# Two matmuls a block instead of three: high weights against both activation parts at once, and a VectorE sum over pairs

## The reference, cut to what matters

```
p = h @ w_in                         # RWKV inputs; then the recurrence
x = x + gt1 * (mix @ w_out)
y = conv3(h @ w_up); x = x + gt2 * ((silu(gate) * val) @ w_down)
z = u @ w_in_2                       # q, k, v, conv branch, gates
h = h + (g_a * (y_a @ w_out_a) + g_b * (att @ w_o_attn)) @ w_mix_out
... a second conv feed-forward, and a final norm
```

## Time and profile before

| | |
|---|---|
| median of 3 runs | 2957.46 us (2954.05 to 2957.95) |
| profiled execution | 2959.5 us from its first to its last instruction |
| TensorE busy | 2802.0 us (95%) |
| TensorE weight loads busy | 2634.0 us (89%) |
| VectorE busy | 1603.0 us (54%) |
| ScalarE busy | 1261.7 us (43%) |
| GpSimd busy | 154.5 us (5%) |
| HBM | 551.29 MB read, 187 GB/s over the span |
| chain that ended last | PE 64%, issue 27%, DVE 4%, DMA 3%, POOL 1%, ACT 1% |

### The profile page before, as it was taken

How to read it: one execution, slowest core, us unless ns; L and a number is a source line. 1 busy time by engine, 2 the same in 40 slices (tenths; PEclk the granted TensorE clock), 3 DMA queues, 4 the chain that set the end, 5 groups by cost and what they waited for, 6 DMA issues and landing times.

```text
span 2959.5 us, 61527 instructions
## 1 busy us (share of the span) xinstructions
PE 2802.0 (95%) x24076; PEld 2634.0 (89%) x24076; DVE 1603.0 (54%) x2138; ACT 1261.7 (43%) x1697; POOL 154.5 (5%) x159
## 2 busy tenths in 40 slices
PE   5799898889899999999979999999989999999997
PEld 0477777769899999999979999999989999999997
DVE  0445454534666666655554565556466666665444
ACT  1432222124555555544434345654455555554443
POOL 1001101131000000001110000000100000000000
PEclk8799999969899999999989999999999999999998
DMA  9675555405345555555545544445535555555553
GB/s 404 274 297 215 214 216 213 193 26 180 138 181 184 184 183 181 178 184 197 201 148 184 180 164 157 159 166 184 184 143 183 184 184 182 177 181 183 199 199 113
DMA packets 76132, 554.88 MB, mean 187 GB/s; under 512 B 8448, under 2 KB 8576, under 8 KB 9088
## 3 DMA queue, kind: packets, MB, share of 16 engines
q1 hardware_dynamic: 75456, 549.16, 50.6%
q10 hardware_dynamic: 432, 2.16, 0.2%
q0 software_dynamic: 144, 2.10, 0.2%
HBM read 551.29 MB, written 2.10 MB: 187 GB/s over the span
## 4 chain that ended last, share of the span: by engine, by line
PE 64%; issue 27%; DVE 4%; DMA 3%; POOL 1%; ACT 1%; DVEq 0%; SPq 0%; POOLq 0%; ACTq 0%
PE bank L428 18%; PE bank L430 18%; PE bank L429 18%; DMA raw<-in_stream_dram 3%; PE bank L461 2%; PE bank L577 1%; PE bank L591 1%; PE bank L587 1%; PE bank L672 1%; PE bank L540 1%; POOL ssq L1750 1%; DVE wlo L1235 0%; POOL wssq L1747 0%; PE bank L644 0%; PE bank L648 0%
## 5 line engine op out<-in xcount | busy, mean ns | idle before, releaser
L428 PE MATMUL bank<-ahi,whi 128*128 128x256 f32 x4976 | 1434.8, 288 | 53.4 <-DVE alo L1263 36.0
L429 PE MATMUL bank<-alo,whi 128*128 128x256 f32 x4976 | 1416.1, 285 | 0.0
L430 PE MATMUL bank<-ahi,wlo 128*128 128x256 f32 x4976 | 1415.6, 284 | 0.0
L1235 DVE TENSOR_TENSOR wlo<-raw,whi 128x1024 fp32r<-128x1024 f32 x846 | 1027.4, 1228 | 262.3 <-ACT whi L889 257.2
L889 ACT ACTIVATE whi<-raw 128x1024 fp32r<-128x1024 f32 x846 | 892.0, 1055 | 572.0 <-PE bank L430 459.7
L428 PEld LDWEIGHTS bank<-ahi,whi 128*128 128x128 f32 x4976 | 962.5, 193 | 85.8 <-issue 69.5
L429 PEld LDWEIGHTS bank<-alo,whi 128*128 128x128 f32 x4976 | 963.6, 194 | 2.8 <-issue 2.6
L430 PEld LDWEIGHTS bank<-ahi,wlo 128*128 128x128 f32 x4976 | 963.2, 194 | 0.0
L428 PE MATMUL bank<-ffhi,whi 128*128 128x256 f32 x1408 | 400.5, 284 | 8.3 <-DVE fflo L1541 8.3
L430 PE MATMUL bank<-ffhi,wlo 128*128 128x256 f32 x1408 | 398.6, 283 | 0.0
L429 PE MATMUL bank<-fflo,whi 128*128 128x256 f32 x1408 | 398.4, 283 | 0.0
(11 more groups left out here) (227 smaller groups left out, 1666.5 us busy)
## 6 DMA issues: line engine op xcount, KB each, us to landing
raw<-in_stream_dram SPq DMA_DIRECT2D x519, 1024.0 KB, 4.8
x<-in_x_dram SPq DMA_DIRECT2D x1, 2048.0 KB, 13.3
out_dram<-x POOLq DMA_DIRECT2D x1, 2048.0 KB, 6.7
lora_w<-in_lora_dram SPq DMA_DIRECT2D x1, 1536.0 KB, 11.2
pool_w<-in_pool_w_dram ACTq DMA_DIRECT2D x1, 1024.0 KB, 9.4
catt<-in_att_dram ACTq DMA_DIRECT2D x1, 576.0 KB, 3.8
par<-in_params_dram SPq DMA_DIRECT2D x1, 541.5 KB, 3.9
pool_inv<-in_pool_inv_dram ACTq DMA_DIRECT2D x1, 512.0 KB, 14.0
```

The source lines that it names most:

```text
L428: nc.tensor.matmul(tile_bank(t), wh, hi[:, kt], start=starts and n == 0, stop=False)
L429: nc.tensor.matmul(tile_bank(t), wh, lo[:, kt], start=False, stop=False)
L430: mm = nc.tensor.matmul(tile_bank(t), wl, hi[:, kt], start=False, stop=stops and last)
L1235: nc.vector.tensor_tensor(wlo[:, k % RING], raw[:, r % RING, 8 * (k % 2):8 * (k % 2) + 8], whi[:, k % RING].bitcast(F32), ALU.subtract).th ...
```

## The change

The high and low activation parts of one feature tile now lie side by side (`act2`, `ff2`, `ya2`, `oa2`), so that one matmul of 512 columns multiplies the high weights with both; it fills a whole bank. The low weights times the high part go into the bank's second half. A tile is the sum of the two halves, so whatever read a tile from PSUM now needs a sum: VectorE's `join` adds the halves, as a reduction over pairs that lie 256 values apart, into SBUF (`joined` or the final place), and the operations behind it read that. In `residual_tile`, two operations take the place of one instead. The bank is given back with the join (`tile_sum`). In `up` ScalarE's and VectorE's taps move one step later, behind the join, and read SBUF; silu, gate, high and low move by a step. `down` waits for the hidden tiles in three portions.

```diff
+        act2 = sb("act2", [P, KT, 2, T], F32R)
+        ahi, alo = act2[:, :, 0], act2[:, :, 1]
...
-                    nc.tensor.matmul(tile_bank(t), wh, hi[:, kt], start=starts and n == 0, stop=False)
-                    nc.tensor.matmul(tile_bank(t), wh, lo[:, kt], start=False, stop=False)
-                    mm = nc.tensor.matmul(tile_bank(t), wl, hi[:, kt], start=False, stop=stops and last)
+                    nc.tensor.matmul(tile_bank(t), wh, flat(pair[:, kt]), start=starts and n == 0, stop=False)
+                    mm = nc.tensor.matmul(small_half(t), wl, pair[:, kt, 0], start=False, stop=stops and last)
...
-                    pe.wait_ge(tile_free, t + 1 - banks + dt * i)
+                    pe.wait_ge(tile_sum, t + 1 - banks + dt * i)
...  down, TensorE
                         for c in range(3):
+                            if j == 0:
+                                pe.wait_ge(ff_ready, which * NF + min(DKT * c + DKT, NF))
...
-            pe.wait_ge(ff_ready, NF)
-            down("down1")
+            down("down1", 0)
...  VectorE
+            def join(dst, phase, j, i=0, per=0):
+                dve.wait_ge(half_used, 2 * FIRST_CHUNK[phase] + (j + 1) * HALVES[phase] + HALVES[phase] * per * i)
+                halves = tile_bank(FIRST_TILE[phase] + j).rearrange("p (h t) -> p t h", h=2)
+                nc.vector.tensor_reduce(dst, halves, AX.X, ALU.add).then_inc(tile_sum, 1)
...  wkv_body, VectorE, step n
-                    if n % 2 == 1 and n // 2 < 6:
-                        j = n // 2
+                    j = n // 2
+                    if n % 2 == 1:
+                        t = FIRST_TILE["wkv"] + j
+                        join(joined[:, t % 2] if j < 6 else one(mix, NR + j - 6 + 2 * i), "wkv", j, i, 8)
+                    if n % 2 == 1 and j < 6:
                         dve.wait_ge(scaled, SCALED["wkv"] + j + 1 + 6 * i)
...  wkv, ScalarE
-                    nc.scalar.activation(dst, tile_bank(t), ACT.Identity, scale=col(om_mu, 3 + 8 * (j // 2) + j % 2 + 2 * i))\
-                        .then_inc(scaled, 1)
-                else:
-                    nc.scalar.activation(one(mix, NR + j - 6 + 2 * i), tile_bank(t), ACT.Copy).then_inc(tile_free, 1)
+                act.wait_ge(tile_sum, t + 1 + 8 * i)
+                nc.scalar.activation(dst, joined[:, t % 2], ACT.Identity, scale=col(om_mu, 3 + 8 * (j // 2) + j % 2 + 2 * i))\
...  residual_tile
+                link(add(small_half(t)))
+                add(large_half(t)).then_inc(tile_sum, 1)
...  up, VectorE
                     for n in range(8):
                         lead(phase, n, i, 4)
+                        if n % 2 == 1:
+                            join(joined[:, n // 2 % 2], phase, n // 2, i, 4)
+                        elif n:
+                            taps_of(n // 2 - 1, i)
...  ao, VectorE
-                    nc.vector.tensor_tensor(yb[:, 2 * part + n % 2], tile_bank(t), one(gates, ct + KT * (n % 2)), ALU.mult)\
-                        .then_inc(tile_free, 1)
+                    join(yb[:, 2 * part + n % 2], "ao", n, i, 8)
+                    dve.wait_ge(tile_sum, t + 1 + 8 * i)
+                    link(nc.vector.tensor_tensor(yb[:, 2 * part + n % 2], yb[:, 2 * part + n % 2], one(gates, ct + KT * (n % 2)),
+                                                 ALU.mult))
```

More of the change, by code:

```diff
@@ L87 @@
     _n += TILES[_name]
+HALVES = {"lora": 2, "wkv": 2, "up1": 2, "qkv": 2, "cvb": 2, "gates": 2, "ao": 1, "up2": 2}
 PARAMS = [("c", KT), ("b_ada", 6 * KT), ("norm1_g", KT), ("mu", 27), ("w0", NR), ("a0", NR), ("k_k", NR), ("k_a", NR),
@@ L416, in _, with product @@
         def _(pe):
-            def product(k, i, dh, t, blocks, hi, lo, starts, stops, ready=None):
+            def product(k, i, dh, t, blocks, pair, starts, stops, ready=None):
                 pe.wait_ge(lo_ready, k + 1 + dh * i)
@@ L864, in _ @@
                     tile_wait(t, i, 8)
-                    hi, lo = (yahi, yalo) if n % 2 == 0 else (oahi, oalo)
-                    product(k, i, 8, t, [(b, b) for b in range(8)], hi, lo, True, True)
+                    pair = ya2 if n % 2 == 0 else oa2
+                    product(k, i, 8, t, [(b, b) for b in range(8)], pair, True, True)
             loop("mix", 4, 4, "gmix")
@@ L869, in _ @@
             loop("up2", 4, 22, "u2")
-            pe.wait_ge(ff_ready, 2 * NF)
-            down("down2")
+            down("down2", 1)
             stat("x5")
@@ L1542, in low, with taps_of @@
                                             ALU.subtract).then_inc(ff_ready, 1)
+                def taps_of(j, i):
+                    dve.wait_ge(scaled, SCALED[phase] + j + 1 + 4 * i)
+                    for m, (tap, back) in enumerate(taps):
+                        dst, src = (slice(back, T), slice(0, T - back)) if back > 0 else (slice(0, T + back), slice(-back, T))
+                        ins = nc.vector.scalar_tensor_tensor(out=yb[:, j, dst], in0=joined[:, j % 2, src],
+                                                             scalar=pcol(conv, 3 * j + tap + 12 * i), in1=yb[:, j, dst],
+                                                             op0=ALU.mult, op1=ALU.add)
+                        if m == 0:
+                            link(ins)
+                    ins.then_inc(tapped, 1)
                 def body(i, first=False):
@@ L1694, in body @@
                         cut_lo(2 * FIRST_CHUNK["gates"] + 32 * kv + n + 2, i, 8, 4)
+                        if n % 2 == 1:
+                            j = 16 * kv + n // 2
+                            join(one(gates, j + 4 * i), "gates", j, i, 4)
                         attend(n, i, kv)
```

165 lines of the change are left out of this document (81 added, 84 removed).

## The result

The changed kernel takes 2919.1 us (median of 4 runs, 2914.2 to 2930.1) where the kernel before took 2957.5 (median of 3 runs, 2954.1 to 2958.0): ratio 0.988, 95% interval 0.985 to 0.990. A fourth run of the kernel before took 5393.7 us and is left out. The changed kernel is faster by 1.2%, not by the forecast 4.7%, and lies outside the range. The profiled execution has a span of 2928.3 us.

A forecast was written before the change was run, and what follows sets the result against it. TensorE's matmul rhythm was taken to bound the dense phases. Terms -138 (blocks), -2.5 (`wkv`), -11 (`up` to `down`), +9 (`ao`), +1.6 (`gates`), +2 (tails) gave -139 from 2959.5: 2820.5, median 2818 us; range 2785 to 2895.

The forecast's parts named there:

- What a block costs: Dense phases: a block falls from 360 to 336 ns, 24 less; over 5760 blocks 138 us off.
- I take that for the new matmul of 512 columns: Block price: the 0.216 us between plain float32 matmuls is taken as the float32r cost at 512 columns.
- 13 ns of the 120 are something else: 256-column matmuls: columns alone would take 107 ns at full clock; the rest was put down to the longer, overlapping weight load.
- a fixed 13 ns per matmul: Rival on block cost, chance 0.15: a block saves 13.3 ns, 77 us in all, time 2885.
- the prediction is wrong if 512 columns take over 0.227: Failure sign for the dense phases: a 512-column matmul was expected to be followed after 0.216 us.
- the half clock: Objection to the fixed-cost rival: at 1.2 GHz 256-column matmuls follow at 0.21 us, showing nothing beyond the columns.
- `wkv`: Per pass with recurrence, 2.9 us of longer waits against 3.1 saved in blocks; 2.5 us off in all.
- `ao`: VectorE becomes the bound at 6.36 us a pair of tiles: 102 us for 92, 9 on.
- the two rivals on it: VectorE's join: slow over short pairs, chance 0.05, time 3000; or between 0.9 and 1.3, chance 0.10, time 2830 to 2850.
- From `up` to `down`: Waiting in portions removes most of two 4.1 us waits and 2.3 us of dropped clock each: 11 us off.
- The third half that was to be 0.85 late: In `down`, VectorE cuts the third half at about 5.9 us, TensorE wants it at 5.04: 0.85 left.
- `gates` and tails: Join before the softmax's division in `gates`, 1.6 us on; one more dependent VectorE operation ending four residual phases, 2 on.

The follow-up runs named there:

- m1_rates: Kernel of its own without the reference's work, rows of 64 single matmuls varied in width and type: float32r takes 0.227 us for 512 columns, 0.120 for 256.
- m2_pairs: Kernel of its own, float32r matmuls of 512 and 256 columns in turn, banks, weights and grouping varied: 346.7 or 353.3 ns a pair.
- three matmuls: Changed kernel with its 512-column matmul replaced by two of 256, joins and all else kept: 2977.2 us, ratio 1.006.

## Why the prediction was wrong, point by point

- **What a block costs: wrong, and it decides.** The step that failed is "I take that for the new matmul of 512 columns": 0.216 from plain float32 of the earlier trace rows. The runs showed in its place that float32r has 227 alone and 230 to 241 in turn (`m1_rates`, `m2_pairs`), so a block is 347 to 353 ns instead of 336, and saves 7 to 13 ns and not 24. Where only the merge differs (the columns "changed" and "three matmuls" of the table) the phases without `wkv` and `ao` gain 53 us, of the 138 forecast. If 13.3 ns had been saved in all 5760 blocks it would be 77; the rest is that `up1`, `up2` and `wout` ran at 353 ns a block in this execution (`up1` 507.0, where 347 brings it to 497) and the `down` phases and `gates` at 350.
- **The step from "13 ns of the 120 are something else" to the load** went wrong: it took the load for the longer of two that overlap, and nothing was left for a fixed part. The first two matmuls of a half did lie 0.22 apart, but the plain float32 row could not tell a hidden load from a type with a smaller constant. With narrower weights 512 columns stay at 230. The rival "a fixed 13 ns per matmul" had the mechanism, and "the prediction is wrong if 512 columns take over 0.227" was the right test. Its 2885 was missed because it had only 3 us for `wkv` and because of the blocks in turn. What counted against it, the half clock, is true (0.43 for 512 columns there, nothing over) and yet says nothing on the full clock.
- **`wkv`: the waits right, the clock left out.** Forecast 2.5 off, measured 16.4 on, of which the four passes have 1.5, 6.6, 4.6 and 3.7. The second pass, the first with a recurrence, takes 123.3 us for 116.7 from its first matmul to the next pass's. The waits for `tinvt`, `us`, `rs` (the second) and `yb` grew by 0.76, 0.76, 0.76 and 0.73: 3.0 where 2.9 was forecast. The blocks save less than thought, 0.05 us in each of 16 halves (3.01 for 3.06: a block takes 352 ns there for 359): 0.7 for 3.1. Some 1.7 are the low clock behind the wait for `us`: from the end of that wait to the end of the second one for `rs` it is 33.3 us for 30.9, of which 0.76 is the longer wait. The 2.6 left lie about the change of passes, 8.9 for 6.3 us from the end of the wait for `yb`, where the stretch at clock 0.5 is 13.7 us long and was 6.8. (3.0 + 1.7 + 2.6 - 0.7 = 6.6.) That stretch differs from execution to execution, and how much of it the longer wait for `yb` causes stays open. With three matmuls and the same waits the clock doesn't fall inside this pass, and it takes 120.5; one execution can't tell whether the merge has a part in that.
- **`ao`: right.** 101.6 for 92.2, forecast 102; VectorE is the bound at 6.46 a pair. The join at 0.69 was right too, which excludes the two rivals on it.
- **From `up` to `down`: right**, 12.4 us for 11. The third half that was to be 0.85 late is 0.16 late: the idle of 8.3 is 0.3.
- **`gates` and tails: small, somewhat more.** The merge left out, `gates` costs 1.3 (216.2 against 214.9; forecast 1.6), and with what `wout`, `qkv`, `mix`, `up` and `down` lose to joins and the second residual operation it comes to some 8 us (three matmuls against before, the 12.4 of the portions added), for the 3.6 forecast.
- **The sum.** -53 for -138 in the blocks, +16 for -2.5 in `wkv`, +9.4 for +9, -12.4 for -11, +8 for +3.6: -32 for -139, and the profiled spans differ by 31. The terms for `ao` and the portions were right by their mechanism; what failed are the blocks, by 85 us, and `wkv`, by 19.

## What to carry to other kernels

Before two matmuls are merged, measure the wider one in the very type and width, or price it with the constant that the same type shows: the gain was the constant saved, here 13 ns less what two widths in turn give back, and not the load that seemed exposed. Give the merge only to phases in which TensorE sets the pace; where another engine is one operation from being the bound (`ao`), or where two engines take turns (`wkv`), what the merge adds on that engine counts whole. And where TensorE's wait is made longer, price the clock behind it as well: here it fell behind a wait of 1.7 us that had been 0.9, and cost 1.5 us more.

## What the runs showed of the hardware

- Float32r matmuls at clock 1.0 follow each other after 120, 173 and 227 ns for 256, 384 and 512 columns: a column a cycle and 13.3 ns. Weights of 64 columns instead of 128 give 113 and 230 for 256 and 512. Bf16 has 109 for 256, plain float32 429 for 512. At clock 0.5 float32r shows nothing over the columns (0.21 and 0.43, in the changed kernel from 358.9 us on).
- 512 and 256 columns in turn cost 347 or 353 ns a pair, each for long stretches and with the same code; `down1` and `down2` have 350 in every kernel with the two in turn. The same code of `up1` took 497 us in the execution of one kernel and 507 in another's through this alone. The runs of a kernel with merged matmuls spread by up to 1% (2890.0 to 2917.7), those of the kernel before by 0.1 to 0.3%.
- VectorE's sum over pairs, 512 values of PSUM into 256 of SBUF, takes 0.69 us, as a copy of 512 to 512 does; an operation on 256 takes 0.42.
- Between the changes of pass in `wkv`, TensorE's waits of 1.7 and 0.87 us had a stretch of granted clock 0.5 (1.2 GHz) behind one of them in six of nine passes, and waits of 0.9 and 0.1 at the same places in one of fifteen. Such a stretch cost a half 1.5 us (4.55 for 3.0).
